# Weight splits ahead of the chunk's hook on ScalarE and VectorE in a 560-chunk transformer kernel

## The chip, the cores and the metric

The kernel runs on one core of a Trainium2 chip. The metric is the device time of one execution in microseconds, the median of several executions.

## What is computed

All inputs and weights are fp32, the sequence has S = 256 positions and the model width is D = 2048. Three layers follow each other on the same x, and a final RMS norm closes the program:

```
first block:  h = rms_norm(x) * (1 + scale) + shift          # scale, shift, gate from silu(c) @ w_ada
              q,k,v,z (two kinds) = split(h @ w_in)
              oa = stick_breaking(rms(q), rms(k), v) * silu(z)
              ob = group_norm(retention(rotary(q), rotary(k), v)) * silu(z)
              x  = x + gate * (concat(oa, ob) @ w_out)
even layer:   proj = rms_norm(x) @ w_in0
              y_a = sc_b * conv(sc_c * sc_v) * silu(sc_z)
              y_b = group_rms(ssd(silu(conv(ssd_xbc)), dt) * silu(ssd_z))
              y_m = memory_attention(mq, mem) * silu(mz)
              x   = x + concat(y_a, y_b, y_m) @ w_out0
odd layer:    latent attention (16 heads, rope) * silu(z_c), memory attention * silu(mz)
              x   = x + concat(y_c, y_m) @ w_out1
out = rms_norm(x)

stick_breaking, per head:
  z = q @ k.T / sqrt(d)
  w = exp(log_sigmoid(z) + sum of log_sigmoid(-z) over the keys between) on past keys, else 0
  out = w @ v
```

## The kernel before

**Weights.** Every projection is a `Gemm` over chunks of weights, 560 chunks in all, most of 128 x 1024 fp32 (512 KB). SyncE's queue loads a chunk into one of seven `raw` slots. ScalarE copies it, rounded, to one of five `w_hi` slots (`split_hi`, line 414). VectorE subtracts the two and writes the rest, `w_lo`, over the raw slot (`split_lo`, line 418). TensorE then multiplies a chunk in pairs of a 512-column and a 256-column matmul (lines 484 and 485), which gives nearly the accuracy of fp32.

**Who waits for whom.** `split_hi` of chunk n waits until its raw data landed and until TensorE has used chunk n - 5. `split_lo` waits for `split_hi` of the same chunk. TensorE waits for `split_lo` of a chunk before its first matmul of it. Both engines run their splits three chunks ahead (`AHEAD = 3`): while TensorE is at chunk i, they split chunk i + 3.

**Hooks.** What is not a projection (attention, convolutions, the SSD scan, norms, gates) is put between the chunks by hooks. A hook is called with the block or pair of heads s and a position p from 0 to 15; the chunk with index i of such a group of eight owns the positions 2i and 2i + 1. On ScalarE and VectorE the order of a step is written by `run_split` (line 420): with `hook_first` set, it is hook(2i), split of chunk i + 3, hook(2i + 1), and, at a block's last chunk, the copy (line 453) or sum (lines 1181, 1186, 1201) that takes the block's products out of PSUM. Without `hook_first` the split stands ahead of both hooks. On TensorE an even hook stands in the middle of the chunk's matmuls and an odd one at its end. Each engine runs its queue in the written order; nothing is reordered by a scheduler.

**Stages.** In time: memory projections and the first chunks of `w_in` (`G_MEM`, `G_SBQK0`, `G_RTQK0`, `G_SBV0`), stick-breaking (`G_RTQK`, `G_RTV`, hook `sb_hook`), retention and gates (`G_SBZ`, `G_RTZ`), `G_OUT`; then the even layer with its convolutions (`G_X0`, `G_DT`, `G_X1`, `G_SZ0`, `G_SZ1`), the SSD scan (`G_M`, `G_CZ`), the late stage (`G_CV`, `G_CC`, hook `late_hook`), `G_CB`, `G_OUT0`; then the odd layer (`G_C1`, `G_C2`, `G_KR`, `G_M1`, `G_UQ`, the key and value stages, `G_ZC`, `G_OUT1`). `G_MEM`, `G_SBQK0`, `G_RTQK0`, `G_SBV0`, `G_X1`, `G_SZ0` and the key and value stages pass `hook_first=False` themselves; all others take the default.

**Stick-breaking, one pair of heads** (period about 29.4 us). TensorE's score products into `psH` (lines 1886, 1887) at p = 7; VectorE adds the mask and takes the magnitude (`L1307`, `L1309`) at p = 8; ScalarE applies exp and log (`L784`, `L786`) at p = 9; VectorE combines them (`L1312`) at p = 11; TensorE sums over the keys (`L1893`) at p = 12. Beside this, VectorE adds up the adaLN gate (`L1228`).

**Late stage, one group of four channel tiles and one memory head** (period about 26.3 us). ScalarE's `log_part` (lines 706 to 708) at p = 0, VectorE's `L1172` at p = 2, ScalarE's exp `L713` at p = 4, VectorE's products `L1532`, `L1533` at p = 6, ScalarE's squares `L926` and the softmax exps `L936` at p = 8, VectorE's normalisation `L1552`, `L1554` at p = 10, and TensorE's transposes `L1807` at p = 10, which wait for them.

Of the kernel before, what the change touches and what calls it, by code (L numbers as in the profile page):

```python
# [147 lines left out]
def build(nc, io):  # L148
    with ExitStack() as ctx:
# [270 lines left out]
        def run_split(eng, split, g, hook, hook_first, block_done):  # L420

            for i, (b, c) in enumerate(g.order):
                s, p = g.position(i)
                if hook_first:
                    hook(s, p)
                if g.c0 + i + AHEAD < len(CHUNKS):
                    split(eng, g.c0 + i + AHEAD)
                if not hook_first:
                    hook(s, p)
                hook(s, p + 1)  # L430
                if i == g.last[b]:
                    block_done(b)
# [9 lines left out]
        def take_product(act, g, b):  # L442

            if g.residual or g.adds:
                return
            products_done(act, g, b)
            if g.tokens:
                out, src = g.tokens(b), psG[:, set_of(g, b):set_of(g, b) + 2, :]
                if len(out.shape) == 4:
                    src = src.rearrange("p h (t d) -> p h t d", t=4)  # L450
                nc.scalar.activation(out, src, ACT.Copy).then_inc(scalar_landed, 1)
            elif g.bias is None or g.norm:
                nc.scalar.activation(g.dst(b), product(g, b, 0), ACT.Copy).then_inc(copied, 1)  # L453
            else:
                nc.scalar.activation(g.dst(b), product(g, b, 0), ACT.Identity, bias=g.bias).then_inc(copied, 1)
# [163 lines left out]
        def _(act):  # L619
# [96 lines left out]
                for n in range(AHEAD):  # L716
                    split_hi(act, n)

            def run(g, hook=no_hook, hook_first=True, before_taken=lambda: None):

                def block_done(b):
                    before_taken()
                    take_product(act, g, b)

                run_split(act, split_hi, g, hook, hook_first, block_done)
# [36 lines left out]
            for i, g in enumerate(G_MEM):  # L762
                run(g, at_units(8 * i, mem_hook_1), hook_first=False)
            for i, g in enumerate((G_SBQK0, G_RTQK0, G_SBV0)):
                run(g, at_units(16 * i, early_hook), hook_first=False)
            run(G_SBQK)
            run(G_SBV)
            landed(act, G_SBQK)
# [265 lines left out]
            for u in range(4):  # L1034
                for half, g in enumerate((G_UK[u], G_UV[u])):
                    run(g, lambda b, p: mem_hook(4 + u, psH[:, BC, :], psH[:, BD, :], 4 * half + p, 2, 5),
                        hook_first=False)
# [71 lines left out]
        def _(dve):  # L1109
# [53 lines left out]
                for n in range(AHEAD):  # L1163
                    split_lo(dve, n)

            def run(g, hook=no_hook, hook_first=True, gate=None):

                run_split(dve, split_lo, g, hook, hook_first, lambda b: add_product(g, b, gate))

# [99 lines left out]
            for i, g in enumerate(G_MEM):  # L1269
                run(g, ada_hook(8 * i, MEM_UNITS, 0), hook_first=False)  # L1270
            for i, g in enumerate((G_SBQK0, G_RTQK0, G_SBV0)):
                run(g, ada_hook(16 * i, EARLY_UNITS, 1), hook_first=False)
# [9 lines left out]
            def gate_columns(half):  # L1282
                dve.wait_ge(q["gate_cols"], half + 1)
                c = 32 + 8 * half
                link(v.tensor_tensor(mod[:, c:c + 8], psH[:, BD, c:c + 8], V("b_ada", c, 8), ALU.add))

            run(G_SBQK, gate_hook(G_SBQK))
            run(G_SBV, gate_hook(G_SBV))
            gate_columns(0)
# [950 lines left out]
```

## Time and profile before

| | us |
|---|---|
| runs | 1802.9, 1805.3, 1808.76 |
| median | 1805.3 |
| the profiled execution | 1803.28 |
| its span | 1801.5 |
| TensorE busy | 1750.1 |
| VectorE busy | 1290.0 |
| ScalarE busy | 899.0 |

The profile shows one execution. Its own time is 1.8 us above its span. An engine's busy time is the sum of its instructions; in the timelines a bracket behind a row gives how long the engine sat idle before that instruction and what released it.

### The profile page before, as it was taken

The numbers are of one execution on the slowest core, as the hardware profiler recorded it, in microseconds if no ns is written. First come the engines' busy times: TensorE is split into PE (matmuls) and PEld (weight loads), VectorE is DVE, ScalarE is ACT, GpSimd is POOL, SyncE is SP. The second block draws the span as 40 slices with busy tenths as digits, with TensorE's granted clock in tenths as the row PEclk, the third lists the DMA queues.
The fourth block names the chain that finished last, engine by engine and source line by source line (L and its number), as shares of the span: only waits on it lengthen the run. The fifth ranks groups of instructions, "written<-read, shape, count | busy, mean of one in ns | idle before, by whom it ended". The sixth has DMA issues, their size and how long they took to land.

```text
span 1801.5 us, 24340 instructions
## 1 busy us (share of the span) xinstructions
PE 1750.1 (97%) x9667; PEld 1498.1 (83%) x9667; DVE 1290.0 (72%) x1634; ACT 899.0 (50%) x1158; POOL 120.3 (7%) x147
## 2 busy tenths in 40 slices
PE   5899999999999999999999999999999999999997
PEld 4788888777888888888888888788888888888885
DVE  6888978785677756888677676975554667778654
ACT  4444443444456445665344666644444545566531
POOL 2411101000010100001000000000000000000000
PEclk9999999999999999999999999999999999999998
DMA  9989979774555566666555555566566565444562
GB/s 324 361 310 331 345 225 324 234 251 134 149 152 164 187 176 187 186 180 184 164 142 142 158 156 167 164 191 188 183 189 180 157 202 144 140 129 129 175 187 94
DMA packets 311889, 350.70 MB, mean 195 GB/s; under 512 B 11248, under 2 KB 286832, under 8 KB 311776
## 3 DMA queue, kind: packets, MB, share of 16 engines
q1 hardware_dynamic: 297792, 298.34, 55.1%
q0 software_dynamic: 13984, 50.80, 8.0%
q8 instruction: 78, 1.28, 0.3%
q14 instruction: 35, 0.29, 0.1%
HBM read 347.00 MB, written 2.10 MB: 194 GB/s over the span
## 4 chain that ended last, share of the span: by engine, by line
PE 73%; DVE 15%; ACT 6%; issue 3%; DMA 2%; POOL 0%; SPq 0%; ACTq 0%; DVEq 0%
PE psG L484 40%; PE psG L485 20%; DVE w_lo L418 4%; ACT w_hi L414 3%; PE psG L478 2%; PE psG L480 2%; PE psG L479 2%; PE psH L1818 1%; DMA raw<-in_mem_w 1%; DVE P L1186 1%; DVE P L1181 1%; PE psH L1832 1%; PE psH L1807 1%; DMA raw<-in_w_in 0%; DVE P L1501 0%
## 5 line engine op out<-in xcount | busy, mean ns | idle before, releaser
L484 PE MATMUL psG<-xA,w_hi 128*128 128x512 f32 x2624 | 948.6, 405 | 3.1 <-DVE w_lo L418 2.5
L418 DVE TENSOR_TENSOR w_lo<-raw,w_hi 128x1024 fp32r<-128x1024 f32 (+1 forms) x560 | 690.0, 1243 | 252.4 <-ACT w_hi L414 251.0
L485 PE MATMUL psG<-xA,w_lo 128*128 128x256 f32 x2624 | 736.5, 281 | 0.0
L414 ACT ACTIVATE w_hi<-raw 128x1024 fp32r<-128x1024 f32 (+1 forms) x560 | 569.4, 1043 | 233.1 <-PE psG L485 167.8
L484 PEld LDWEIGHTS psG<-xA,w_hi 128*128 128x128 f32 x2624 | 493.7, 188 | 126.0 <-issue 8.8
L485 PEld LDWEIGHTS psG<-xA,w_lo 128*128 128x128 f32 x2624 | 496.4, 189 | 4.2 <-issue 3.4
L484 PE MATMUL psG<-yP,w_hi 128*128 128x512 f32 x960 | 338.5, 396 | 3.5 <-DVE P L1186 1.6
L485 PE MATMUL psG<-yP,w_lo 128*128 128x256 f32 x960 | 269.2, 280 | 0.0
L484 PEld LDWEIGHTS psG<-yP,w_hi 128*128 128x128 f32 x960 | 179.9, 187 | 46.3 <-DVE P L1186 1.9
L453 ACT ACTIVATE P<-psG 128x512 f32<-128x512 f32 (+2 forms) x103 | 60.9, 592 | 251.0 <-PE psG L485 251.0
L485 PEld LDWEIGHTS psG<-yP,w_lo 128*128 128x128 f32 x960 | 181.4, 189 | 0.2
L1181 DVE TENSOR_TENSOR P<-psG,P 128x512 f32<-128x512 f32 (+2 forms) x103 | 70.4, 684 | 116.8 <-ACT P L453 116.8
L1228 DVE SCALAR_TENSOR_TENSOR ada_sum<-ada_ring,silc,ada_sum 128x1024 f32<-128x1024 f32 x60 | 77.9, 1303 | 0.0
L592 POOL DMA_DIRECT2D ada_ring<-in_w_ada x96 | 50.8, 530 | 323.3 <-DVE ada_sum L1228 132.5
L581 POOL TENSOR_TENSOR W<-W 128x512 f32<-128x512 f32 x15 | 26.1, 1741 | 651.9 <-ACT W L636 651.9
L1201 DVE TENSOR_TENSOR xT<-psG,xT 128x512 f32<-128x512 f32 x32 | 22.1, 692 | 54.1 <-PE psG L485 53.5
L484 PE MATMUL psG<-xM,w_hi 128*128 128x512 f32 x128 | 47.5, 412 | 5.4 <-DVE xM L1126 4.8
L478 PE MATMUL psG<-w_hi,xA 128*128 128x512 f32 x128 | 52.1, 407 | 0.0
L484 PE MATMUL psG<-xQ,w_hi 128*128 128x512 f32 x144 | 51.1, 399 | 0.0
L479 PE MATMUL psG<-w_lo,xA 128*128 128x512 f32 x128 | 50.5, 395 | 0.0
L480 PE MATMUL psG<-w_hi,xA 128*128 128x512 f32 x128 | 50.4, 394 | 0.0
L485 PE MATMUL psG<-xQ,w_lo 128*128 128x256 f32 x144 | 40.4, 281 | 0.0
(318 smaller groups left out, 1761.5 us busy)
## 6 DMA issues: line engine op xcount, KB each, us to landing
raw<-in_w_in SPq DMA_DIRECT2D x360, 512.0 KB, 3.8
raw<-in_w_out SPq DMA_DIRECT2D x128, 512.0 KB, 3.5
ada_ring<-in_w_ada POOLq DMA_DIRECT2D x96, 512.0 KB, 6.3
raw<-in_mem_w SPq DMA_DIRECT2D x32, 512.0 KB, 8.8
raw<-in_w_uq SPq DMA_DIRECT2D x24, 384.0 KB, 3.3
raw<-in_w_ukv SPq DMA_DIRECT2D x32, 128.0 KB, 2.5
raw<-in_w_ukv SPq DMA_DIRECT2D x16, 256.0 KB, 3.4
P<-in_memT SPq DMA_DIRECT2D x4, 512.0 KB, 5.8
```

Source lines behind the costliest of these rows:

```text
L414: nc.scalar.activation(high(n), low(n, raw), ACT.Copy).then_inc(hi_ready, 1)
L418: nc.vector.tensor_tensor(low(n), low(n, raw), high(n), ALU.subtract).then_inc(lo_ready, 1)
L453: nc.scalar.activation(g.dst(b), product(g, b, 0), ACT.Copy).then_inc(copied, 1)
L478: nc.tensor.matmul(out, x_hi, hi[:, w], start=first, stop=False)
L479: nc.tensor.matmul(out, x_hi, lo[:, w], start=False, stop=False)
L480: last = nc.tensor.matmul(out, x_lo, hi[:, w], start=False, stop=end)
L484: nc.tensor.matmul(psG[:, bank + f, :], hi[:, w], x, start=first, stop=False)
L485: last = nc.tensor.matmul(psG[:, bank + f, S:2 * S], lo[:, w], x[:, 0:S], start=False, stop=end)
L581: nc.gpsimd.tensor_tensor(a[:, 0:512], a[:, 0:512], a[:, 512:1024], ALU.add).then_inc(q["nm_pair"], 1)
L592: pool.dma_start(ada_ring[slot][:, :], ada_rows(k, part, half)).then_inc(ada_loaded[slot], 16)
L1181: ins = v.tensor_tensor(out, product(g, b, 1), out, ALU.add)
L1228: v.scalar_tensor_tensor(out=out, in0=src, scalar=silc[:, k:k + 1], in1=out, op0=ALU.mult, op1=ALU.add).then_inc(ada_used, 1)
```

## The change

The default of `hook_first` goes from true to false in ScalarE's `run` and in VectorE's `run`. In every stage that took the default, the split of chunk i + 3 now stands ahead of the hook of the even position 2i, on both engines. The stages that passed false themselves are as before, and so is TensorE's, SyncE's and GpSimd's order. No instruction, buffer or semaphore is added or taken away.

```
--- before.py
+++ after.py
@@ -716,7 +716,7 @@
                 for n in range(AHEAD):
                     split_hi(act, n)
 
-            def run(g, hook=no_hook, hook_first=True, before_taken=lambda: None):
+            def run(g, hook=no_hook, hook_first=False, before_taken=lambda: None):
 
                 def block_done(b):
                     before_taken()
@@ -1163,7 +1163,7 @@
                 for n in range(AHEAD):
                     split_lo(dve, n)
 
-            def run(g, hook=no_hook, hook_first=True, gate=None):
+            def run(g, hook=no_hook, hook_first=False, gate=None):
 
                 run_split(dve, split_lo, g, hook, hook_first, lambda b: add_product(g, b, gate))
```

VectorE in the stick-breaking stage, the first pair of heads. `L1228` is the gate's sum, `L1201` takes a block's products, `work_73` holds the scores z:

```order
 L1228 SCALAR_TENSOR_TENSOR gate_sum<-ada_ring_68,silc,gate_sum 128x1024
 L1201 TENSOR_TENSOR P<-psG,P 128x512 x2
+L418 TENSOR_TENSOR w_lo<-raw,w_hi 128x1024
 L1307 TENSOR_TENSOR work_73<-psH,con_72 128x768
 L1309 SCALAR_TENSOR_TENSOR work_73<-work_73 128x768
-L418 TENSOR_TENSOR w_lo<-raw,w_hi 128x1024 x2
+L418 TENSOR_TENSOR w_lo<-raw,w_hi 128x1024
 L1312 SCALAR_TENSOR_TENSOR work_73<-work_73 128x768
```

One split (of the group's chunk 7) has moved from behind `L1309` to ahead of `L1307`; the split of chunk 8 stands ahead of `L1312` in both.

ScalarE in the late stage, first group, before:

```order
L453 ACTIVATE P<-psG 128x512
L706 ACTIVATE W<-P 128x1024
L707 ACTIVATE W<-W 128x1024
L708 ACTIVATE W<-W 128x1024
L414 ACTIVATE w_hi<-raw 128x1024 x2
L713 ACTIVATE W<-W 128x1024
L414 ACTIVATE w_hi<-raw 128x1024 x2
L453 ACTIVATE P<-psG 128x512
L926 ACTIVATE W<-P 128x1024
L936 ACTIVATE P,col<-psH,col 128x256 x2
```

and the same stretch of ScalarE after:

```order
L453 ACTIVATE P<-psG 128x512
L414 ACTIVATE w_hi<-raw 128x1024
L706 ACTIVATE W<-P 128x1024
L707 ACTIVATE W<-W 128x1024
L708 ACTIVATE W<-W 128x1024
L414 ACTIVATE w_hi<-raw 128x1024 x2
L713 ACTIVATE W<-W 128x1024
L414 ACTIVATE w_hi<-raw 128x1024
L453 ACTIVATE P<-psG 128x512
L414 ACTIVATE w_hi<-raw 128x1024
```

The split of chunk 3 has moved ahead of `log_part` (`L706` to `L708`), and that of chunk 7 to ahead of `L926`.

VectorE in the same group, from its second split to the normalisation, with `L1181` and `L1186` taking a block's products:

```order
 L1532 TENSOR_TENSOR W<-P,W 128x1024
 L1533 TENSOR_TENSOR P<-P,W 128x1024
-L418 TENSOR_TENSOR w_lo<-raw,w_hi 128x1024
-L1181 TENSOR_TENSOR P<-psG,P 128x512
-L1186 TENSOR_TENSOR P<-P,con 128x512
-L418 TENSOR_TENSOR w_lo<-raw,w_hi 128x1024
+L1181 TENSOR_TENSOR P<-psG,P 128x512
+L1186 TENSOR_TENSOR P<-P,con 128x512
+L418 TENSOR_TENSOR w_lo<-raw,w_hi 128x1024 x2
 L1552 RECIPROCAL col<-col 128x2
 L1554 TENSOR_SCALAR P<-P,col 128x256 x2
```

The split of chunk 6, which stood behind `L1533`, stands ahead of `L1532` now, and `L1552` has the splits of chunks 7 and 8 ahead of it where it had that of chunk 7.

## Rows read from the trace of the kernel before

**Rows 1.** The page's first part: busy time and share of each engine.

```profile
PE 1750.1 (97%) x9667; PEld 1498.1 (83%) x9667; DVE 1290.0 (72%) x1634; ACT 899.0 (50%) x1158; POOL 120.3 (7%) x147
```

**Rows 2.** TensorE's waits by releaser: total us, times, longest.

```profile
PE psG L484 <- DVE w_lo L418: 3.5, 4, 2.1
...
PE psH L1893 <- DVE work L1312: 2.5, 3, 1.0
...
PE psG L484 <- DVE P L1186: 1.6, 1, 1.6
PE psH L2010 <- DVE P L1509: 1.2, 4, 0.3
PE psG L484 <- DVE yP L1770: 1.0, 1, 1.0
...
PE psH L1807 <- DVE P L1709: 0.5, 1, 0.5
PE psG L484 <- DVE yP L1388: 0.4, 1, 0.4
...
PE psH L1932 <- DVE work L1347: 0.2, 1, 0.2
```

**Rows 3.** The page's costliest groups: count, busy and mean ns, idle before and releaser.

```profile
L418 DVE TENSOR_TENSOR w_lo<-raw,w_hi 128x1024 fp32r<-128x1024 f32 (+1 forms) x560 | 690.0, 1243 | 252.4 <-ACT w_hi L414 251.0
```

**Rows 4.** Timeline of VectorE, first pair of heads: start us, us, instruction, idle before.

```profile
336.87 0.95 DVE L1307 TENSOR_TENSOR work<-psH,con 128x768 f32<-128x768 f32 x1
337.85 0.96 DVE L1309 SCALAR_TENSOR_TENSOR work<-work 128x768 f32<-128x768 f32 x1
338.72 1.22 DVE L418 TENSOR_TENSOR w_lo<-raw,w_hi 128x1024 fp32r<-128x1024 f32 x1
341.55 1.23 DVE L418 TENSOR_TENSOR w_lo<-raw,w_hi 128x1024 fp32r<-128x1024 f32 x1 [1.60 <-ACT w_hi L414]
342.69 0.95 DVE L1312 SCALAR_TENSOR_TENSOR work<-work 128x768 f32<-128x768 f32 x1
```

**Rows 5.** Timeline of ScalarE, the same stretch.

```profile
338.84 0.85 ACT L784 ACTIVATE work<-work 128x768 f32<-128x768 f32 x1 [5.91 <-DVE work L1309]
...
340.47 1.99 ACT L414 ACTIVATE w_hi<-raw 128x1024 fp32r<-128x1024 f32 x2
```

**Rows 6.** Timeline of TensorE: its sums over keys, first and third pair of heads.

```profile
343.70 0.91 PE L1893 MATMUL psH<-work,con 128*128 128x384 f32 x2 [0.90 <-DVE work L1312]
...
402.49 0.91 PE L1893 MATMUL psH<-work,con 128*128 128x384 f32 x2 [0.96 <-DVE work L1312]
```

**Rows 7.** Timeline of VectorE, fourth pair of heads.

```profile
424.14 0.96 DVE L1307 TENSOR_TENSOR work<-psH,con 128x768 f32<-128x768 f32 x1 [1.37 <-PE psH L1887]
```

**Rows 8.** Timeline of ScalarE, first group of the late stage.

```profile
1004.39 1.05 ACT L706 ACTIVATE W<-P 128x1024 f32<-128x1024 f32 x1
...
1007.53 1.99 ACT L414 ACTIVATE w_hi<-raw 128x1024 fp32r<-128x1024 f32 x2
```

**Rows 9.** Timeline of VectorE, the same group.

```profile
1009.82 1.22 DVE L1172 SCALAR_TENSOR_TENSOR W<-P,W 128x1024 f32<-128x1024 f32 x1
...
1019.71 1.23 DVE L418 TENSOR_TENSOR w_lo<-raw,w_hi 128x1024 fp32r<-128x1024 f32 x1 [0.51 <-ACT w_hi L414]
...
1021.04 0.62 DVE L1554 TENSOR_SCALAR P<-P,col 128x256 f32<-128x256 f32 x2
```

**Rows 10.** Timeline of TensorE, its transposes in the first and last late group.

```profile
1021.72 0.54 PE L1807 MATMUL psH<-con,P 128*128 128x128 f32 x3
...
1100.74 0.66 PE L1807 MATMUL psH<-con,P 128*128 128x128 f32 x4
```

**Rows 11.** Windows: length, busy of PE, PEld, DVE, ACT, POOL, then granted clock.

```profile
402.00:405.00 3.00, 2.51 (x11) 1.88 (x12) 3.00 (x4) 0.00 (x0) 0.00 (x0) 1.00 0.79 277
1142.00:1144.00 2.00, 1.14 (x3) 1.04 (x4) 2.00 (x5) 1.94 (x3) 0.00 (x0) 0.67 0.75 256
1144.00:1146.00 2.00, 2.00 (x8) 1.65 (x7) 0.66 (x2) 2.00 (x3) 0.00 (x0) 0.50 0.00 0
```

More of the change, by code:

```diff
@@ L717, in first, with run @@
                     split_hi(act, n)
-            def run(g, hook=no_hook, hook_first=True, before_taken=lambda: None):
+            def run(g, hook=no_hook, hook_first=False, before_taken=lambda: None):
                 def block_done(b):
@@ L1164, in first, with run @@
                     split_lo(dve, n)
-            def run(g, hook=no_hook, hook_first=True, gate=None):
+            def run(g, hook=no_hook, hook_first=False, gate=None):
                 run_split(dve, split_lo, g, hook, hook_first, lambda b: add_product(g, b, gate))
```

## The prediction

> **What bounds the kernel now.** I read the page's first part before anything else. TensorE is busy 97% of the span, VectorE 72%, ScalarE 50% [rows 1], so an edit that adds no instruction can matter only through TensorE's idle time. The second view is TensorE's waits by releaser [rows 2]. Those that this edit can reach, since they are on results of VectorE in stages that change their order, are the rows shown: 3.5 + 2.5 + 1.6 + 1.2 + 1.0 + 0.5 + 0.4 + 0.2 = 10.9 us. That is all there is to win, 0.6% of the span. The third view is VectorE's largest group: before its 560 subtractions (`L418`) VectorE sat idle 252.4 us, nearly all of it until ScalarE's rounding copy (`L414`) [rows 3]. It looks like much, but TensorE's four waits on `w_lo` are only 3.5 us of it [rows 2]: the splits run three chunks ahead, and their lateness is absorbed. So the splits are the work with slack, and the hooks, whose results TensorE wants at a fixed position, are mostly the work without it. Putting the former ahead of the latter gives slack to who has it already. The last view is the timeline of the three engines at each place where a hook's chain ends in a wait of TensorE, or just fails to.
>
> **Stick-breaking: three waits grow.** The chain of a pair of heads is VectorE `L1307`, `L1309`, ScalarE `L784`, `L786` and its split of chunk 8, VectorE's split of chunk 8, `L1312`, TensorE `L1893`. VectorE comes to `L1307` without any idle time, that is late [rows 4]; ScalarE has idled 5.91 us when `L1309` releases it [rows 5]; TensorE waits 0.90 us at the first pair and 0.96 us at the third [rows 6], and three such waits make the 2.5 us [rows 2]. Before, VectorE did its split of chunk 7 at 338.72, while ScalarE did `L784` and `L786`: it was hidden there, and VectorE idled another 1.60 us after it [rows 4]. Now it stands ahead of `L1307`. Its cost is from its start to the next one's, 1.14 us (341.55 to 342.69) [rows 4]. All later steps are released one by another, so all shift by that: 3 x 1.14 = 3.4 us. In the fourth pair VectorE idled 1.37 us before `L1307` for TensorE's scores [rows 7]; the split falls into this hole, and costs nothing. Bounds for the stage: 0 if ScalarE or TensorE ahead of it give the time back, 4 x 1.14 = 4.6 us if the hole is gone too, since the pair before ends later.
>
> **Late stage: a wait that isn't there yet.** Here ScalarE takes its split of chunk 3 ahead of `log_part`, whose first part starts at 1004.39, with the two splits behind it at 1007.53 [rows 8]. Two splits take 1.99 us, and a later one starts about 0.95 us behind the one before. The chain from there is `log_part`, VectorE `L1172` (1009.82) [rows 9], ScalarE's exp, VectorE's `L1532` and `L1533`, ScalarE's `L926` and `L936`, its split of chunk 8, then the same split on VectorE, `L1552`, `L1554`, and TensorE's transposes. Each step waits for the one before, so it all moves by some 0.95 us. At its end `L1554` starts at 1021.04 and lasts 0.62 us, to 1021.66 [rows 9]; TensorE's `L1807` starts at 1021.72 [rows 10]. The cover is 0.06 us. There are four groups, 26.3 us apart (from 1021.72 to 1100.74 in three steps) [rows 10]. TensorE's list has no large wait there now; after the change it waits about 0.95 us in each: 3.8 us. Bounds: 0 if the chain has slack in its middle which I don't see, 4 x (0.95 + 1.14) = 8.4 us if VectorE's additional split ahead of `L1552` adds to ScalarE's. I take 3.8, since VectorE idled 0.51 us ahead of the split at 1019.71 [rows 9], and so a part of its own split fits.
>
> **Gains.** In the gate stage after stick-breaking, VectorE's split of chunk 4 waited for ScalarE's, which stood behind `log_part`; now ScalarE does it earlier, and the wait on `L1347` (0.2 us) goes [rows 2]. At the start of `G_OUT`, `yP` (`L1388`) comes about two splits' time earlier than TensorE's 0.4 us wait on it: -0.4. At the end of the latent attention and the start of `G_OUT1` two waits, 0.5 on `L1709` and 1.0 on `L1770`, lie behind chains in which a split goes ahead of some steps and behind others; I take -0.7, bounds -1.5 and +1.1 (one split more). Together -1.3 us.
>
> **Edits that cost nothing.** In the SSD scan VectorE's split moves into a time when it waits for ScalarE; the wait of TensorE on `L1509`, 1.2 us in four, stays [rows 2]. At the passage to `G_OUT0` the waits on `w_lo` (3.5 us, the longest 2.1) and on `L1186` (1.6) [rows 2] come from the sum of work of both engines there, not from its order: if the earlier waits shrink, TensorE comes sooner to the chunk that waits for `L1186`, and waits that much longer. 0, with bounds -3 and +2. The moves in `G_M1`, `G_UQ` and `G_OUT1` lie in chains with more than a chunk of slack: 0. In the latent attention a VectorE split goes ahead of `L1709` beside a `log_part` in three places; TensorE waits there only once, 0.5 us [rows 2]: 0, with a bound of 3 x 1.14 = 3.4 us if no cover is left in any. No DMA issue changes its place on a queue. SyncE's loads wait for TensorE to use a chunk, which is unchanged.
>
> **The sum.** 3.4 + 3.8 - 1.3 = +5.9 us. The profiled execution took 1803.28 us, so it would be 1809.2 there; the median of the runs is 2.0 us higher, 1805.3, and 1805.3 + 5.9 = 1811.2. I predict 1811.
>
> **A rule beside it.** After waits of TensorE near 1 us the granted clock stays at 1.00, as in the window from 402 to 405 [rows 11]. After the longest one, 2.1 us on `w_lo` [rows 2], it shows 0.67 and then 0.50, the level of 1.2 GHz instead of 2.4 [rows 11]. The Trainium skill, "TensorE: Matmul & The Clock Gate", section "A second HAM failure mode: psum-queue depth-cycling", holds that small idle times between groups of matmuls, if frequent, make the clock swing between its two levels. The trace does not agree for waits of this size and distance (1.00 after 0.96 us), but by that rule the new waits would cost more than their length.
>
> **Rival 1, the covers hold; within 0.3%.** If the late stage has slack that I miss, only stick-breaking and the gains count: 3.4 - 1.3 = +2.1, 1807.4 us. For it speaks that I add up a chain of ten steps to within 0.06 us; against it that rows 9 and 10 show the end just met in both the first and the last group. With neither stage's loss it is 1804.
>
> **Rival 2, faster.** The mechanism is the transition to `G_OUT0`: with splits first, `w_lo` is no longer late, the 3.5 us go, and so does the slow clock behind the longest of them. In the two windows that costs 0.33 x 2.0 + 0.50 x 2.0 = 1.7 us [rows 11]. With the gains of 1.3 and some of `L1186` it gives -6.5 to -8, and if stick-breaking is as I say and the late stage costs nothing, 1805.3 + 3.4 - 7 = 1802; with neither loss 1798. It decides if VectorE's splits there are late by their place, and not by the work. For it: ScalarE's `log_part` and eight convolution steps do stand ahead of splits there. Against: both engines are nearly full.
>
> **Rival 3, the clock.** In the third pair of heads the wait becomes 0.96 + 1.14 = 2.1 us, as long as the one that dropped the clock. Each drop costs 1.7 us by rows 11: one gives 1811.2 + 1.7 = 1812.9, one in each of the three pairs 1816.3, and with the late stage's four, 1823.
>
> **Rival 4, latent attention.** If the copies of `L1709` are each late by a whole split, +3.4; I take two thirds of it for what cover there is, +2.3: 1813.5. For it: `L1709` is in the list of waits already [rows 2]. Against: 0.5 us in a single wait isn't a chain late at every turn.
>
> **How the numbers follow.** Chances: the forecast (1808.5 to 1812.5) 0.45; rival 1 (1804 to 1808.5) 0.22; rival 2 (1797 to 1803) 0.12; rival 3 0.12; rival 4 0.09. A measurement of this kernel can tell about 0.3%, 5.4 us, from no change: the bounds are 1799.9 and 1810.7. Of rival 2 two thirds lie under the lower one. Of the forecast some 60% lies above the upper one, and all of rivals 3 and 4: 0.27 + 0.12 + 0.09 = 0.48 slower. Faster 0.08, same 0.44. The range runs from 1803, which leaves out rival 2, to 1817, which leaves out the clock in more than three places.
>
> **What would show it.** TensorE's waits: on `L1312` 2.5 us to about 5.9, with the fourth pair as before; a new row `L1807` on `L1554` of nearly 4 us in four waits; `L1347` and `L1388` gone; on `L1509` still 1.2. VectorE's busy time stays, and its idle time ahead of `L418` falls, without use. I am wrong if `L1807` stays out of the list, if the waits from 1109 to 1165 shrink by more than 2 us in all, or if the clock's row shows more than one place at half level.

## The result

| | before | after |
|---|---|---|
| median of the runs, us | 1803.61 (18 runs) | 1813.46 (18 runs) |
| lowest and highest | 1795.21, 1808.76 | 1808.37, 1818.04 |
| span of the profiled execution | 1801.5 | 1806.6 |

The ratio is 1.0048 with a 95% interval of 1.0037 to 1.0059: slower by 8.7 us (6.7 to 10.6); the two medians alone are 9.85 us apart. The forecast was +5.9 us and 1811. Before has more runs here than the three of the prediction, and its median is 1.7 us lower.

The first part of the page of the changed kernel, and its largest groups (busy and mean ns; idle before, and releaser). They answer to [rows 1] and [rows 3]:

```profile
PE 1747.2 (97%) x9667; PEld 1496.1 (83%) x9667; DVE 1283.6 (71%) x1634; ACT 901.4 (50%) x1158; POOL 112.7 (6%) x147
...
L418 DVE TENSOR_TENSOR w_lo<-raw,w_hi 128x1024 fp32r<-128x1024 f32 (+1 forms) x560 | 684.7, 1235 | 239.8 <-ACT w_hi L414 237.6
```

The same work is done. VectorE waits 238 us for ScalarE's copies where it waited 251, and this buys nothing: TensorE's waits are longer. By releaser, in the changed kernel (total us, times, longest), to be read against [rows 2]:

```profile
PE psH L1893 <- DVE work L1312: 5.8, 3, 2.1
...
PE psG L484 <- DVE w_lo L418: 3.9, 4, 1.7
...
PE psG L484 <- DVE P L1186: 3.4, 2, 2.3
...
PE psH L1807 <- DVE P L1554: 1.7, 4, 0.4
PE psH L2010 <- DVE P L1509: 1.3, 4, 0.4
PE psG L484 <- DVE yP L1770: 1.0, 1, 1.0
PE psH L1807 <- DVE P L1440: 0.9, 1, 0.9
PE psH L1880 <- ACT W L775: 0.9, 1, 0.9
...
PE psH L1807 <- DVE P L1709: 0.2, 1, 0.2
```

`L1312` has grown from 2.5 to 5.8 us, as its chain said. `L1554`, `L775`, `L1440` and a second wait on `L1186` are new. `L1388` and `L1347` are gone. The splits themselves (`w_lo`), which the change puts first, are waited for about as long as before.

**Stick-breaking.** VectorE, ahead of the scores of the first pair of heads:

```profile
333.04 1.41 DVE L1201 TENSOR_TENSOR P<-psG,P 128x512 f32<-128x512 f32 x2
334.36 1.21 DVE L418 TENSOR_TENSOR w_lo<-raw,w_hi 128x1024 fp32r<-128x1024 f32 x1
335.49 0.95 DVE L1307 TENSOR_TENSOR work<-psH,con 128x768 f32<-128x768 f32 x1
...
340.18 1.23 DVE L418 TENSOR_TENSOR w_lo<-raw,w_hi 128x1024 fp32r<-128x1024 f32 x1 [2.74 <-ACT w_hi L414]
341.32 0.95 DVE L1312 SCALAR_TENSOR_TENSOR work<-work 128x768 f32<-128x768 f32 x1
```

and TensorE's first wait for it:

```profile
342.32 0.59 PE L1893 MATMUL psH<-work,con 128*128 128x384 f32 x1 [1.79 <-DVE work L1312]
```

The split of chunk 7 takes 1.13 us (334.36 to 335.49) that the chain would have had. VectorE gets the same time back as idle time, 2.74 us where there were 1.60 [rows 4], at a place where it is of no use. TensorE's wait is 1.79 us where it was 0.90 [rows 6].

**Late stage.** The same points of the first group in the changed kernel, ScalarE, VectorE, TensorE:

```profile
1004.65 1.05 ACT L414 ACTIVATE w_hi<-raw 128x1024 fp32r<-128x1024 f32 x1
1005.60 1.05 ACT L706 ACTIVATE W<-P 128x1024 f32<-128x1024 f32 x1
```

```profile
1010.96 1.22 DVE L1172 SCALAR_TENSOR_TENSOR W<-P,W 128x1024 f32<-128x1024 f32 x1
...
1020.84 1.23 DVE L418 TENSOR_TENSOR w_lo<-raw,w_hi 128x1024 fp32r<-128x1024 f32 x1 [0.52 <-ACT w_hi L414]
...
1022.18 0.61 DVE L1554 TENSOR_SCALAR P<-P,col 128x256 f32<-128x256 f32 x2
```

```profile
1022.85 0.33 PE L1807 MATMUL psH<-con,P 128*128 128x128 f32 x1 [0.43 <-DVE P L1554]
```

Against [rows 9 and 10], `L1172` stands 1.14 us later, `L1554` 1.14 and `L1807` 1.13. About 0.2 us of that was there when the stage began in this execution, so the chain itself lost some 0.9 us. TensorE's list shows only 0.43 of it; most of the rest is a wait on `L926` ahead of it, 0.3 us a group, which is under the size that the list names. The sum over the four groups is read from the distance of the first `L1807` from the last: 79.02 us before [rows 10], 81.72 after (1022.85 to 1104.57), so 0.90 us a group, and 3.5 to 3.6 us for four.

### The profile page after: what moved, and what is told of

Read it like the earlier page. It is cut to its first block, busy times and chain, and to the rows that moved or that the text cites. A ratio compares the mean times of both kernels' runs of the same rounds, so it can differ in the third digit from the quotient of the medians.

```text
span 1806.6 us, 24338 instructions
## 1 busy us (share of the span) xinstructions
PE 1747.2 (97%) x9667; PEld 1496.1 (83%) x9667; DVE 1283.6 (71%) x1634; ACT 901.4 (50%) x1158; POOL 112.7 (6%) x147
## 4 chain that ended last, share of the span: by engine, by line
PE 75%; DVE 13%; ACT 5%; issue 3%; DMA 2%; POOL 0%; SPq 0%; ACTq 0%; DVEq 0%
PE psG L484 40%; PE psG L485 20%; DVE w_lo L418 5%; ACT w_hi L414 3%; PE psG L478 2%; PE psG L480 2%; PE psG L479 2%; PE psH L1818 1%; DMA raw<-in_mem_w 1%; DVE P L1181 1%; DVE P L1186 1%; PE psH L1807 1%; DMA ada_ring<-in_w_ada 1%; PE psH L1832 1%; DVE P L1461 1%
## 5 line engine op out<-in xcount | busy, mean ns | idle before, releaser
L1181 DVE TENSOR_TENSOR P<-psG,P 128x512 f32<-128x512 f32 (+2 forms) x103 | 70.4, 684 | 132.4 <-ACT P L453 132.1
L1228 DVE SCALAR_TENSOR_TENSOR ada_sum<-ada_ring,silc,ada_sum 128x1024 f32<-128x1024 f32 x60 | 77.8, 1301 | 0.1
L581 POOL TENSOR_TENSOR W<-W 128x512 f32<-128x512 f32 x15 | 22.0, 1469 | 664.7 <-ACT W L636 664.7
L1201 DVE TENSOR_TENSOR xT<-psG,xT 128x512 f32<-128x512 f32 x32 | 22.1, 691 | 54.3 <-PE psG L485 53.8
```

Source lines behind the costliest of these rows:

```text
L1181: ins = v.tensor_tensor(out, product(g, b, 1), out, ALU.add)
L1201: ins = v.tensor_tensor(x, src, x, ALU.add)
L1228: v.scalar_tensor_tensor(out=out, in0=src, scalar=silc[:, k:k + 1], in1=out, op0=ALU.mult, op1=ALU.add).then_inc(ada_used, 1)
```

## The experiments

Ratios are against the kernel before, with 95% intervals, and a difference in us is the ratio's, unless it says otherwise. Experiments 1 and 2 do one stage alone, 3 and 4 one engine alone. Most intervals are some 6 us wide, so the size of a single stage is read from the traces.

### 1. Stick-breaking alone

```
-            run(G_RTQK, sb_hook)
+            run(G_RTQK, sb_hook, hook_first=False)
...
-            run(G_RTQK, both(sb_hook, gate_hook(G_RTQK)))
+            run(G_RTQK, both(sb_hook, gate_hook(G_RTQK)), hook_first=False)
```

`G_RTV` is changed in the same way, on both engines.

> The kernel before, with the split ahead of the even hook on both engines in the stick-breaking stage alone (G_RTQK, G_RTV). My theory: VectorE's split ahead of L1307 delays three of four pairs by 1.14 us each, so TensorE's wait on L1312 goes from 2.5 to about 5.9 us, and ScalarE's split ahead of L774/L775 in the third pair's place adds 0.9 us on L775, as in the changed kernel: +4.3 us in all. Rival: these waits are only moved there, and with the other stages unchanged the time is given back later: +1 us or less. Second rival: the longest wait, 2.1 us, lowers the TensorE clock: +1.5 us more.

Measured: 1806.42 us, ratio 1.0022 (1.0004 to 1.0040), +4.0 us. TensorE's waits:

```profile
PE psH L1893 <- DVE work L1312: 6.0, 3, 2.1
...
PE psH L1880 <- ACT W L775: 0.9, 1, 0.9
```

By the trace the stage costs what the chain said (3.5 us on `L1312` and 0.9 on `L775`), and of the later waits only the 0.4 us on `L1388` is missing from the list. The timed interval, 0.7 to 7.2 us, agrees, but would by itself just allow the first rival. The second rival holds once in this profile: the clock drops behind the first pair's wait and not behind the third's (rows below, under "The clock"). The wait on `L775` comes from ScalarE's half: its split now stands ahead of the squares `L774`, `L775`, for which TensorE waits once.

### 2. The late stage alone

```
-            run(G_CV, late_hook)
-            run(G_CC, lambda b, p: late_hook(2 + b, p))
+            run(G_CV, late_hook, hook_first=False)
+            run(G_CC, lambda b, p: late_hook(2 + b, p), hook_first=False)
```

> The kernel before, with the split ahead on both engines in the late stage alone (G_CV, G_CC). My theory: each of the four groups loses 0.85 to 0.95 us on L926 and L1554, about +3.5 us, and the delay is permanent. Rival: the late stage's loss comes only from what the stages ahead of it pass on (a delayed ScalarE): under +1 us. Rival 2: the next stage, in which VectorE and ScalarE bind, absorbs part of it, since TensorE arrives later at waits that are there anyway: +1 to +2 us.

Measured: 1806.50 us, ratio 1.0021 (1.0005 to 1.0037), +3.8 us. Four waits on `L1554` show 1.8 us of it; from the first `L1807` to the last it is 81.88 us (1027.54 to 1109.42) where it was 79.02, so 0.95 us a group. The chain had no more cover than the 0.06 us, and the waits behind the stage (3.3 us on `w_lo`, 1.6 on `L1186`) are about as before: nothing is given back. The timed interval, 0.9 to 6.7 us, excludes the first rival only just and the second not at all; it is the trace that decides against both.

### 3. VectorE's half alone, in these two stages

```
-            run(G_RTQK, both(sb_hook, gate_hook(G_RTQK)))
+            run(G_RTQK, both(sb_hook, gate_hook(G_RTQK)), hook_first=False)
...
-            run(G_CV, late_hook)
+            run(G_CV, late_hook, hook_first=False)
```

The edit is in VectorE's program only, and covers `G_RTV` and `G_CC` too.

> The kernel before, with VectorE's splits alone ahead of the even hooks, in the stick-breaking and the late stage; ScalarE as before. My theory: in stick-breaking it is VectorE's split that costs, so the wait on L1312 is 5.9 us again, without the one on L775. In the late stage VectorE's split of chunk 8 now waits for a ScalarE split that stands behind L700, which waits for TensorE: each group costs some 3.6 us, 14 us in all; together +17 us. Rival: VectorE's part costs only its own splits, 1.14 us a group: +3.4 + 4.6 = +8 us.

Measured: 1831.99 us, ratio 1.0164 (1.0137 to 1.0191), +29.6 us, nearly twice what my own theory had. TensorE's waits:

```profile
PE psH L1807 <- DVE P L1554: 8.9, 4, 2.4
PE psH L2025 <- ACT W L926: 8.7, 4, 2.3
PE psH L1893 <- DVE work L1312: 5.8, 3, 2.1
```

The expected mechanism is there, but it is one of three costs. The first is a wait that I hadn't counted, on `L926` (8.7 us). VectorE ahead of it, in the first group, with the splits of chunks 5 and 6:

```profile
1016.85 1.23 DVE L418 TENSOR_TENSOR w_lo<-raw,w_hi 128x1024 fp32r<-128x1024 f32 x1 [2.07 <-ACT w_hi L414]
...
1018.79 1.22 DVE L418 TENSOR_TENSOR w_lo<-raw,w_hi 128x1024 fp32r<-128x1024 f32 x1
1019.93 1.22 DVE L1532 TENSOR_TENSOR W<-P,W 128x1024 f32<-128x1024 f32 x1
```

The split of chunk 4 stands ahead of `L1172` now and that of chunk 6 ahead of `L1532`, 1.14 us each. Between them ScalarE's exp `L713` comes late, since it waits for `L1172`, and ScalarE's split of chunk 5 behind it; VectorE waits 2.07 us for that one. `L926` starts 15.44 us behind `L706` where it was 12.37. The second cost is the expected one, on `L1554`, 8.9 us where I had 14. ScalarE and VectorE ahead of it:

```profile
1025.58 0.39 ACT L700 ACTIVATE W<-psH 128x256 f32<-128x256 f32 x1 [0.23 <-PE psH L2025]
...
1026.32 1.04 ACT L414 ACTIVATE w_hi<-raw 128x1024 fp32r<-128x1024 f32 x1
```

```profile
1027.39 1.23 DVE L418 TENSOR_TENSOR w_lo<-raw,w_hi 128x1024 fp32r<-128x1024 f32 x1 [0.78 <-ACT w_hi L414]
1028.54 0.15 DVE L1552 RECIPROCAL col<-col 128x2 f32<-128x2 f32 x1
1028.73 0.62 DVE L1554 TENSOR_SCALAR P<-P,col 128x256 f32<-128x256 f32 x2
```

`L1552` needs nothing of the split, but stands behind it; the split needs ScalarE's copy, which stands behind `L700`, which waits for TensorE. The third cost is the clock. It falls to half level once in each group: at the wait on `L1554` that ends at 1029.40, after those on `L926` that end at 1056.3 and 1089.3, and after the one on `L1554` that ends at 1127.30. The first of these in the windows, with the clock as the third number from the end:

```profile
1030.00:1032.00 2.00, 2.00 (x8) 1.73 (x7) 0.00 (x0) 1.45 (x2) 0.00 (x0) 0.50 0.01 4
```

None of the other eleven profiles has such a place in this stage. At the 1.7 us a drop of the prediction they are 6.8 us, and 3.3 + 8.7 + 8.9 + 6.8 = 27.7 us, against 29.6 (24.7 to 34.4) timed. In stick-breaking the wait on `L1312` is the whole 5.8 us with VectorE's half alone, and `L775` isn't in the list.

### 4. ScalarE's half alone, in all stages

```
-            def run(g, hook=no_hook, hook_first=True, before_taken=lambda: None):
+            def run(g, hook=no_hook, hook_first=False, before_taken=lambda: None):
```

> The change on ScalarE alone, in every stage; VectorE as before. My theory: the wait on L1312 stays at 2.5 us and the late stage has no new wait (L1552 isn't behind the split of chunk 8); L775 costs its 0.9 us; and in G_CB VectorE's split of chunk 3 no longer waits behind four ScalarE instructions (L968), which fills 1.1 us of its idle time per half: net -1 to -3 us against before. Rival: in G_CB and G_OUT0 both engines are full and order is worth nothing: +1 us. Rival 2: it is ScalarE's split ahead of log_part that delays the late stage: +3.8 us there.

Measured: 1795.02 us, ratio 0.9953 (0.9935 to 0.9971): 8.5 us **faster** than before, with one half of the same edit. TensorE's waits:

```profile
PE psH L1893 <- DVE work L1312: 2.3, 3, 1.0
...
PE psG L484 <- DVE P L1186: 0.9, 1, 0.9
...
PE psH L1880 <- ACT W L775: 0.9, 1, 0.9
...
PE psG L484 <- DVE w_lo L418: 0.5, 1, 0.5
```

The rows on `L1509`, `L1709`, `L1770`, `L1388` and `L1347` of [rows 2] are gone, and the late stage has no new one: its four `L1807` span 79.09 us (1018.82 to 1097.91), where it was 79.02. The largest part is at `G_CB`. VectorE there before:

```profile
1111.21 1.22 DVE L1580 TENSOR_TENSOR P<-P 128x1024 f32<-128x1024 f32 x1
1115.22 1.23 DVE L418 TENSOR_TENSOR w_lo<-raw,w_hi 128x1024 fp32r<-128x1024 f32 x1 [2.79 <-ACT w_hi L414]
```

and with ScalarE's half:

```profile
1108.44 1.22 DVE L1580 TENSOR_TENSOR P<-P 128x1024 f32<-128x1024 f32 x1
1109.57 1.22 DVE L418 TENSOR_TENSOR w_lo<-raw,w_hi 128x1024 fp32r<-128x1024 f32 x1
1111.44 1.67 DVE L1586 SCALAR_TENSOR_TENSOR W<-P,vec,W 128x255 f32<-128x255 f32 x4 [0.64 <-ACT W L968]
```

ScalarE's four `L968` wait for VectorE's `L1580`. Before, ScalarE's split stood behind them, and VectorE waited 2.79 us for it. With ScalarE's half the copy is ready when VectorE has done `L1580`, so VectorE subtracts while ScalarE does the `L968`: both have work. With VectorE's half on top of it, its split stands ahead of `L1580`, the `L968` come that much later, and the next split waits for ScalarE again.

### 5. The gate sum at other chunks

```
-        GATE_AT = {..., G_RTQK: lambda i: i % 2 == 1, G_RTV: lambda i: i < 8}
+        GATE_AT = {..., G_RTQK: lambda i: i % 2 == 0 or i == 15, G_RTV: lambda i: i < 8 and i != 3}
```

ScalarE's half as in experiment 4, but not in `G_RTQK` and `G_RTV`.

> The change on ScalarE alone, except in stick-breaking, where ScalarE is as before; and VectorE's gate sum (L1228) moved out of the step ahead of L1307 (to the even chunks of G_RTQK, and away from the fourth of G_RTV). My theory: L1307 starts 1.2 us earlier, which is more than TensorE's waits of 0.67 to 0.96 us on L1312, so these three are gone or under 0.3 us in all (-2.3 us), and the wait on L775 is gone (-0.9 us): about 3 us faster than ScalarE's half alone, about 11 us faster than before. Rival: L1307 is bound by L1201 or by TensorE's scores ahead of it: no gain from the gate sum, waits on L1312 stay at 2.3.

Measured: 1791.16 us, ratio 0.9929 (0.9908 to 0.9950), 12.8 us faster than before, and the fastest of all by its median. Its interval and that of experiment 4 overlap, so the times don't show a gain over it. The trace does: TensorE's waits on `L1312` are 1.3 us in two where they were 2.3 in three, and `L775` is gone. The third pair's 0.96 us went, as expected. In the first two pairs 0.66 us stay, and neither my theory nor the rival has the reason. The edit didn't take the sum out of the row of work ahead of `L1307`: it only moved it from behind a split to ahead of it. VectorE works there without idle time (but for 0.28 us) from an `L1201` at 333.57 to `L1307` at 341.39, which is 7.82 us; before it was 7.83 (329.04 to 336.87). Only in the third pair does the row hold one sum less.

### 6. VectorE's half in `G_CB` and `G_OUT0`, on top of ScalarE's half

```
-            run(G_CB, sc_hook)
+            run(G_CB, sc_hook, hook_first=False)
...
-            run(G_OUT0, out0_hook)
+            run(G_OUT0, out0_hook, hook_first=False)
```

> ScalarE's half of the change everywhere, and VectorE's half in G_CB and G_OUT0 alone. My theory: VectorE's split of chunk 3 ahead of L1580 delays ScalarE's four L968 and with them both engines' chain by 1.14 us a half, and the split of chunk 4 makes VectorE wait for ScalarE's behind L968 again: TensorE's waits on w_lo come back, 3 to 4 us of the 3.9 of the changed kernel, with L1186 at 2.3 us and a drop of the clock: +6 to +8 us against ScalarE's half alone, so about as long as before. Rival: the changed kernel's waits there come from TensorE's different arrival and from what was delayed before; then +1 us.

Measured: 1803.73 us, ratio 0.9981 (0.9963 to 0.9998). Against experiment 4 that is 1803.73 - 1795.02 = 8.7 us by the medians, though the two kernels ran beside different runs of before; by the ratios it is 0.28%, 5.0 us, and the two intervals just overlap. The waits:

```profile
PE psG L484 <- DVE w_lo L418: 5.3, 4, 1.7
...
PE psG L484 <- DVE P L1186: 2.4, 1, 2.4
```

Of the 5.3 us, 1.1 lie at 48 us, ahead of anything that was changed; the other three waits, 4.2 us, are at the passage, where experiment 4 had none, and the clock drops once behind the one on `L1186` (0.50 from 1168 to 1170). VectorE's next split behind `L1580` waits 2.72 us for ScalarE again. So the theory's mechanism holds, and not the rival's; the size, +6 to +8 us, is 5.0 by the ratios.

### 7. VectorE's half in `G_M1`, on top of ScalarE's half

```
-            run(G_M1, c_norm_hook)
+            run(G_M1, c_norm_hook, hook_first=False)
```

> ScalarE's half of the change everywhere, and VectorE's half in G_M1 alone. My theory: VectorE's split ahead of L1658, ScalarE's copy behind L1658, its next split behind that copy and VectorE's next split behind that form a ring of about 3.05 us per chunk, where TensorE takes 2.83; over the stage it eats the slack of three chunks and TensorE waits about 1.0 us on L1186: +1 us, visible in the trace only. Rival: the ring is absorbed (my prediction said so), 0 us.

Measured: 1793.80 us, ratio 0.9938 (0.9917 to 0.9959), not to be told from experiment 4 by time. Its trace has the wait, at the same matmul as the changed kernel:

```profile
1422.51 0.50 PE L484 MATMUL psG<-xQ,w_hi 128*128 128x512 f32 x1 [1.10 <-DVE P L1186]
```

In the changed kernel one sees the ring that makes it, VectorE and then ScalarE:

```profile
1422.11 1.22 DVE L418 TENSOR_TENSOR w_lo<-raw,w_hi 128x1024 fp32r<-128x1024 f32 x1 [1.10 <-ACT w_hi L414]
1423.26 0.48 DVE L1658 SCALAR_TENSOR_TENSOR P<-P,vec 128x256 f32<-128x256 f32 x1
...
1425.17 1.22 DVE L418 TENSOR_TENSOR w_lo<-raw,w_hi 128x1024 fp32r<-128x1024 f32 x1 [1.10 <-ACT w_hi L414]
```

```profile
1423.77 0.42 ACT L1024 ACTIVATE xQ<-P 128x256 fp32r<-128x256 f32 x1 [1.69 <-DVE P L1658]
1424.09 1.04 ACT L414 ACTIVATE w_hi<-raw 128x1024 fp32r<-128x1024 f32 x1
```

Split, `L1658`, ScalarE's `L1024`, its split, VectorE's next split: 3.06 us a turn (1422.11 to 1425.17), each engine idle over a third of it. Before, a turn was 1.9 us. TensorE takes about 2.8 us per chunk (eight pairs of matmuls, 1422.20 to 1425.02), so it catches up 0.2 us a turn.

### 8. `log_part` of `G_CB` in ScalarE's idle time, on top of experiment 5

```
+                if n == 3 and p == 14:
+                    log_part(W[:, 1024:2048], tiles(SCZ, 4)).then_inc(q["gate_log"], 1)
...
-                if p == 2:
-                    log_part(W[:, 1024:2048], tiles(SCZ + 4 * v, 4)).then_inc(q["gate_log"], 1)
+                if v == 0 and p == 14:
+                    act.wait_ge(q["sc_done"], 1)
+                    log_part(W[:, 1024:2048], tiles(SCZ + 4, 4)).then_inc(q["gate_log"], 1)
```

> The kernel with ScalarE's half (stick-breaking as before) and the later gate sum, and in addition the two log_part triples of G_CB put into idle time of ScalarE (the first at the end of the late stage, the second at the end of G_CB's first half). My theory: TensorE's last wait at the passage to G_OUT0, 0.9 us on L1186, is bound by VectorE, which has no idle time ahead of it: same time within 1 us. Rival: the wait hangs on ScalarE's log_part, and the 0.9 us go.

Measured: 1794.28 us, ratio 0.9931 (0.9904 to 0.9958), the same as experiment 5. The wait on `L1186` (1.0 us) stayed, as my theory had it.

### 9. The changed kernel with VectorE's half undone in five stages

```
-            run(G_CV, late_hook)
-            run(G_CC, lambda b, p: late_hook(2 + b, p))
+            run(G_CV, late_hook, hook_first=True)
+            run(G_CC, lambda b, p: late_hook(2 + b, p), hook_first=True)
```

So too `G_RTQK`, `G_RTV`, `G_CB`, `G_OUT0` and `G_M1`, in VectorE's program.

> The changed kernel with VectorE's half undone in five places: stick-breaking, the late stage, G_CB, G_OUT0 and G_M1. My theory: these hold nearly all of what separates the changed kernel (1813.5) from ScalarE's half alone (1795): 3.4 + 3.5 + 8 to 9 + 1 = 16 to 17 us. What is left of VectorE's half, in the gate stages, G_OUT, the SSD scan, the latent attention and G_OUT1, costs the waits on L1509 (1.3) and L1770 (1.0): 1796 to 1798, 0.4% under the kernel before. Rival: VectorE's half does more harm where no wait of TensorE names it, and the time stays above 1801.

Measured: 1795.94 us, ratio 0.9976 (0.9958 to 0.9994), 4.3 us faster than before. By the ratios that takes back 0.72% (13 us) of the 0.95% (17 us) between the changed kernel and experiment 4, so the places named hold most of what VectorE's half costs; nearly all, as I expected, is not shown, with intervals of this width. The waits on `L1509` (1.2) and `L1770` (1.0), which ScalarE's half alone had taken away, are there again.

### 10. ScalarE's half in `G_CB` and `G_OUT0` alone

```
-            run(G_CB, sc_hook)
+            run(G_CB, sc_hook, hook_first=False)
...
-            run(G_OUT0, out0_hook)
+            run(G_OUT0, out0_hook, hook_first=False)
```

In ScalarE's program, with all else as before.

> The kernel before with ScalarE's half of the change in G_CB and G_OUT0 alone. My theory: this is where most of ScalarE's gain is. TensorE's waits on w_lo (3 us of the 3.5) and the drop of the clock behind the longest (1.7 us) go, L1186 falls from 1.6 to 0.9: -5 to -5.5 us. The other 2.5 to 3 us of ScalarE's half are in the waits on L1509, L1709, L1770, L1388 and L1347, less 0.9 on L775. Rival: the gain is spread over all stages, and this kernel is only 1 to 2 us faster.

Measured: 1795.54 us, ratio 0.9966 (0.9951 to 0.9982), 6.1 us (3.2 to 8.8) faster than before, by one argument in two places. Its one wait on `w_lo` of 1.4 us lies in the first 50 us, ahead of anything that was changed; at `G_CB` and `G_OUT0` there is none.

## Why the prediction was right, and where not

**The direction and the range held:** 1813.46 in 1803 to 1817, slower by 0.48% where 0.33% was forecast. It lies 1 us above the forecast's own interval (1808.5 to 1812.5), and beside rival 4's 1813.5 by chance alone, as that rival's waits didn't come. The terms, by the waits of the traces:

| term | predicted | measured |
|---|---|---|
| stick-breaking, `L1312` | +3.4 | +3.3 |
| stick-breaking, `L775` | not seen | +0.9 |
| late stage | +3.8 | +3.5 |
| gains | -1.3 | -0.9 (0.4 `L1388`, 0.2 `L1347`, 0.3 `L1709`) |
| `G_CB`, `G_OUT0` | 0 | +1.5 |
| `G_M1` | 0 | +1.1 |
| sum | +5.9 | +9.4, against +8.7 (6.7 to 10.6) timed |

**Stick-breaking** was right step by step, the free fourth pair included, and experiment 3 shows that the cost on `L1312` is VectorE's. I read the chain from `L1307` to `L1893` and no other in the stage, and I let only results of VectorE make waits: ScalarE's split ahead of `L775` is a chain of its own that ends in TensorE's sums of squares.

**The late stage** was right in size, but my reason was half of it. I put the loss on ScalarE's split ahead of `log_part`. ScalarE's half alone has the same split there and loses nothing (experiment 4), since its copy of chunk 7 then comes ahead of `L926`, and VectorE's subtraction ahead of `L1552` no longer waits for it. The loss needs VectorE's half, and with that alone it is several times larger (experiment 3). From the first `L1807` to the last:

| splits ahead in the late stage | us |
|---|---|
| none (before) | 79.02 |
| on ScalarE alone (experiment 4) | 79.09 |
| on both (changed kernel, experiment 2) | 81.72, 81.88 |
| on VectorE alone (experiment 3), three drops of the clock included | 97.90 |

So rival 1, that this stage has slack, fell by experiment 2.

**The step that failed** is the passage to `G_OUT0`. I wrote that its waits "come from the sum of work of both engines there, not from its order". Experiment 10 refutes this: an order in which ScalarE goes first and VectorE doesn't takes 6 us off. Rival 2 had the right mechanism for ScalarE's half. I gave it 0.12 because I took the change as one thing; its two halves work against each other, -8.5 us by experiment 4 and, by the ratios (1.0048 - 0.9953), some +17 us between that and the changed kernel. The net of the place in the changed kernel, from the late stage's last transposes to the wait on `L1186`, is about 1.5 us: TensorE loses 5.9 us in waits where it lost 4.6, and both kernels have one drop of the clock. That my 0 came near this is luck: ScalarE's half takes some 6 us off there (experiment 10) and VectorE's half puts 5 us or more back (experiment 6). The 10.9 us that I called all there is to win also left something out, the clock and the waits under the list's size.

**`G_M1`** failed as a term of slack. I compared the ring with nothing; its turn of 3.06 us against TensorE's 2.8 could have been added up from the durations.

**The clock** (rival 3). In the changed kernel's profile it stays at 1.00 behind all three grown waits on `L1312`, so the rival's drops didn't come there. But how long one wait is doesn't tell whether the clock falls. In experiment 1's profile the first pair's wait was 2.03 us (until 351.48) and the third's 2.09 (until 414.31); the windows behind them (length, busy of PE, PEld, DVE, ACT, POOL, clock):

```profile
353.00:355.00 2.00, 2.00 (x6) 1.39 (x6) 1.97 (x4) 0.00 (x0) 0.44 (x1) 0.50 0.37 74
...
415.00:417.00 2.00, 2.00 (x11) 1.54 (x10) 2.00 (x3) 0.00 (x0) 0.00 (x0) 1.00 0.29 115
```

The very wait on `w_lo` that the prediction read, 2.1 us with a drop behind it [rows 2, 11], is 2.09 us in experiment 1 (until 1154.37), and there the clock reads 1.00 from 1152 to 1160. A drop doesn't need a wait of TensorE either. The same part of the program, in the kernel before and then in the changed one, with TensorE busy since 238 in both (it did 6 and 11 matmuls in these 2 us):

```profile
242.00:244.00 2.00, 2.00 (x6) 1.52 (x6) 1.97 (x6) 1.34 (x4) 0.00 (x0) 0.50 0.01 5
```

```profile
242.00:244.00 2.00, 2.00 (x11) 1.63 (x10) 1.86 (x5) 2.00 (x4) 0.00 (x0) 1.00 0.00 1
```

So a drop in one profile can't be put down to the wait ahead of it. The changed kernel also shows 0.53 and 0.62 from 444 to 448, and 0.50 behind the 2.3 us wait on `L1186` at 1167.75, which follows three other waits within 20 us. By its letter that is the sign that I named, more than one place at half level. It was a poor sign: the kernel before has such places too (above), and the one near 444 stands in nine of the ten experiments' profiles, also where nothing ahead of it was changed (experiment 2). The rule of the Trainium skill that the prediction weighed ("TensorE: Matmul & The Clock Gate", "A second HAM failure mode: psum-queue depth-cycling"), that frequent small idle times make the clock swing, is in keeping with the drops behind rows of waits, here at 1167.75 and in experiment 3. It doesn't account for the one at 242, and no run here changes the number of waits alone.

**Rival 4** fell: `L1709` is waited for 0.2 us, less than before.

## What to carry to other kernels

When two engines each split work between a shared task and their own chains, and the shared task passes from one to the other, the order of the producer and of the consumer are two changes: here the producer (ScalarE) gained by doing its part of the task early, and the consumer (VectorE) lost by it, since its own chain then stood behind a split, and often behind the wait for the producer's. Price each half alone, and build each half alone, before the two. For each hook that a step is moved ahead of, follow its chain to the first wait of the engine that bounds; a loop over both engines costs its whole turn, to be compared with the bound engine's pace.

## What was not expected of the hardware

TensorE's pace differs between executions at the same granted clock. The same stretch of the program, with TensorE busy throughout, in the kernel before and after (third and fourth number: TensorE's busy time and its matmuls):

```profile
600.00:750.00 150.00, 150.00 (x847) 130.10 (x846) 101.13 (x128) 77.34 (x95) 12.71 (x6) 1.00 0.63 182
```

```profile
600.00:750.00 150.00, 150.00 (x859) 131.68 (x858) 98.09 (x127) 79.11 (x96) 9.09 (x6) 1.00 0.64 185
```

These are 847 and 859 matmuls in 150 us, 1.4% apart, while the clock's row reads 1.00 in both. (Both profiles hold 9667 matmuls in all, so records missing from one of them aren't the reason.) From 450 us to the `L1807` at 806, with idle times taken out, it makes about 3.5 us, in favour of the changed kernel. With one drop of the clock fewer in its profile up to 1780 us (1.7 us), it is the larger part of why its profiled span is only 5.1 us above that of before, where the waits say 9.4 and the timed runs 8.7. It isn't the change: the profile of experiment 2 goes at the pace of before there, and those of the others at or near that of the changed kernel. The new wait of 0.9 us on `L1440`, which lies at the end of this stretch, goes with the pace too. It is in every profile except these two at the lower pace, also where these stages are untouched (experiment 1), so I leave it out of the sum. What sets the pace stays open. It and the number of drops make spans of single profiles of this kernel comparable to no better than some 4 us; the waits inside them compare much better.
